# Local attention two heads at a time, normalised only by the head norm, and gated products in idle accumulator banks, in the mixing stages of a two-block kernel

## The reference

```python
for l in range(2):
    h = rms_norm(x, norm_mix_g[l])
    p = h @ w_in[l]
    y_a = silu(layer_norm(causal_conv(p[..., :256] * sigmoid(p[..., 256:o1]))))   # 31 taps
    q, k, v = heads(p[..., o1:o2])                    # 4 heads of 64
    y_b = causal_softmax(q @ k.T / 8) @ v             # one block of 256: plain causal attention
    y_b = y_b * rsqrt(mean(y_b**2, per head) + 1e-6) * moba_out_g[l]
    y_c = gla_chunked(...)                            # gated linear attention, 4 heads of 128
    y_c = y_c * rsqrt(mean(y_c**2, per head) + 1e-6) * gla_out_g[l] * silu(p[..., o6:])
    x = x + concat(y_a, y_b, y_c) @ w_out[l]
    x = x + ffn_with_short_conv(rms_norm(x, norm_ffn_g[l]), ...)
```

## Time and profile before

| | us |
|---|---|
| median of 3 runs (1288.66 to 1292.35) | 1292.04 |
| the profiled execution | 1291.89 |
| its span | 1290.2 |
| PE busy in it | 1255.8 |
| DVE busy | 820.3 |
| ACT busy | 670.9 |
| POOL busy | 144.6 |

### The profile page before, as it was taken

One profiled execution on the slowest core, in us unless ns is written; L12 is line 12 of the kernel. 1 busy time (PEld: TensorE's weight loads), 2 busy tenths in 40 slices (PEclk: granted clock), 3 DMA queues, 4 the chain that ended last, 5 costly groups with the idle time before them and its releaser, 6 DMA issues.

```text
span 1290.2 us, 16634 instructions
## 1 busy us (share of the span) xinstructions
PE 1255.8 (97%) x6276; PEld 1032.7 (80%) x6276; DVE 820.3 (64%) x943; ACT 670.9 (52%) x794; POOL 144.6 (11%) x169
## 2 busy tenths in 40 slices
PE   6999999999999999999989999999999999999997
PEld 5888888888898678888878778888888877888885
DVE  4466455545567665555459877877746987677762
ACT  6554254444455554444346365676526554767651
POOL 2000000000010000000019510000004931000000
PEclk9999999999999999999989999999999999999999
DMA  8544554446364235555523325544562423544440
GB/s 327 219 155 182 184 195 180 171 174 225 131 245 164 95 145 201 195 194 213 196 94 141 132 97 196 195 159 167 196 225 107 164 99 131 196 183 162 177 179 33
DMA packets 31526, 220.13 MB, mean 171 GB/s; under 512 B 3888, under 2 KB 3920, under 8 KB 5488
## 3 DMA queue, kind: packets, MB, share of 16 engines
q1 hardware_dynamic: 29664, 213.92, 44.8%
q0 software_dynamic: 1664, 5.41, 1.3%
q10 hardware_dynamic: 144, 0.04, 0.0%
HBM read 218.30 MB, written 1.05 MB: 170 GB/s over the span
## 4 chain that ended last, share of the span: by engine, by line
PE 92%; DVE 5%; ACT 2%; POOL 1%; issue 1%; DMA 0%; POOLq 0%; ACTq 0%
PE acc L1440 26%; PE acc L1442 26%; PE acc L1441 26%; PE tb L1468 5%; DVE wlo L899 2%; PE acc L1617 1%; PE acc L1619 1%; PE acc L1620 1%; ACT whi L473 1%; DVE cacc L1225 1%; PE tb L1831 1%; PE tb L1531 1%; PE tb L1652 1%; PE tb L1857 0%; PE tb L1671 0%
## 5 line engine op out<-in xcount | busy, mean ns | idle before, releaser
L899 DVE TENSOR_TENSOR wlo<-raw,whi 128x2048 fp32r<-128x2048 f32 x202 | 462.7, 2310 | 240.0 <-ACT whi L473 240.0
L473 ACT ACTIVATE whi<-raw 128x2048 fp32r<-128x2048 f32 x202 | 380.6, 1907 | 110.2 <-PE acc L1442 100.9
L1440 PE MATMUL acc<-whi,xth 128*128 128x512 f32 (+1 forms) x1056 | 419.4, 397 | 8.2 <-DVE wlo L899 6.2
L1442 PE MATMUL acc<-whi,xtl 128*128 128x512 f32 (+1 forms) x1056 | 410.1, 388 | 0.0
L1441 PE MATMUL acc<-wlo,xth 128*128 128x512 f32 (+1 forms) x1056 | 409.3, 388 | 0.0
L1440 PEld LDWEIGHTS acc<-whi,xth 128*128 128x128 f32 x1056 | 199.2, 189 | 53.3 <-issue 8.3
L1442 PEld LDWEIGHTS acc<-whi,xtl 128*128 128x128 f32 x1056 | 199.1, 189 | 41.4
L1441 PEld LDWEIGHTS acc<-wlo,xth 128*128 128x128 f32 x1056 | 199.5, 189 | 37.4
L1440 PE MATMUL acc<-whi,yth 128*128 128x512 f32 x512 | 203.8, 398 | 1.8 <-DVE ytl L1373 1.8
L1442 PE MATMUL acc<-whi,ytl 128*128 128x512 f32 x512 | 200.1, 391 | 0.0
L1441 PE MATMUL acc<-wlo,yth 128*128 128x512 f32 x512 | 199.9, 390 | 0.0
(11 more groups left out here) (230 smaller groups left out, 1005.4 us busy)
## 6 DMA issues: line engine op xcount, KB each, us to landing
raw<-in_stream SPq DMA_DIRECT2D x202, 1024.0 KB, 4.8
rb<-in_rel_rows POOLq DMA_DIRECT2D x8, 256.0 KB, 2.9
x<-in_x_in SPq DMA_DIRECT2D x2, 512.0 KB, 5.8
gs_sb<-in_gs_row POOLq DMA_DIRECT2D x1, 1024.0 KB, 5.5
frow<-in_fin_row POOLq DMA_DIRECT2D x2, 512.0 KB, 5.1
out<-x SPq DMA_DIRECT2D x2, 512.0 KB, 2.6
ws_sb<-in_ws_t POOLq DMA_DIRECT2D x1, 512.0 KB, 4.2
gb_sb<-in_gate_b POOLq DMA_DIRECT2D x2, 128.0 KB, 3.0
```

The costliest lines, as they stand in the source:

```text
L473: act.activation(whi[:, s, :], raw[:, s, :], ACT.Copy).then_inc(hi_ready, 1)
L899: dve.tensor_tensor(wlo[:, s, :], raw[:, s, :], whi[:, s, :], ALU.subtract).then_inc(lo_ready, 1)
L1440: pe.matmul(o, xh, wh, start=first, stop=False)
L1442: return pe.matmul(o, xl, wh, start=False, stop=last)
```

## The change

In both mixing layers:

- **Scores.** The attention goes by pairs of heads, p = 0 and 1. Two heads lie in rows 0 to 63 and 64 to 127 of `mqT`/`mkT`; `moba_scores` alternates between them and writes to two banks, and each DVE instruction, each pair of maxima and each copy then covers two heads. There are two scores places on PE instead of four.
- **No division.** The exponentials are not divided by their sums. The four heads' products lie side by side in `tb[0]`; ACT squares the bank (line 811 of the new file), DVE sums per head, adds EPS times the squared sum of exponentials, POOL takes the root, and one DVE multiply per layer makes `mo`.
- **Banks.** `gla_out(0)` and `gla_out(1)` go to the accumulators of step 4, which are idle then, one right after the other; `y_turn` uses two banks of its own.
- **Order.** The weight splits `lo(U0+11)` and `lo(U0+12)` come later on DVE; the attention is over before `out_product`; unit j = 1 waits for all three remainders instead of two; `mo_turn` stands between units 1 and 2 instead of within unit 2; on ACT the copy of the attention's high part stands ahead of `hi(U0+14)` and `hi(U0+15)` instead of behind them.

```diff
+        pp2 = [at("pp2_0", [2, 384], o_sc + 2112), at("pp2_1", [2, 384], o_sc + 1088)]
+        tball = ctx.enter_context(nc.psum_tensor("tb", [P, 4, 512], F32))
...
                 keep(4, mv, 256)
                 hi(U0 + 11)
-                h_exp(0)
+                moba_exp(0)
                 o_keep(0)
-                h_keep(0)
+                o_keep(1)
+                moba_exp(1)
                 hi(U0 + 12)
+                moba_keep(0)
...
-                o_keep(1)
-
+                keep(5, rs, 512, ACT.Silu, (0,))
                 act.wait_ge(x_sl, 2 * l + 2)
                 act.activation(yth[:, 0:512], ycs[:, :, :].rearrange("p a t -> p (a t)"), ACT.Copy).then_inc(x_yh, 1)
-                keep(5, rs, 512, ACT.Silu, (0,))
-                h_exp(1)
+                moba_keep(1)
+                act.wait_ge(t_o, 2 * l + 2)
+                act.activation(msq[:, :], tb[0], ACT.Square).then_inc(t_sq, 1)
                 keep(5, rs, 512, ACT.Silu, (1,))
...
-                lo(U0 + 11)
...
+                def moba_begin(p):
+                    i = 2 * l + p
+                    dve.wait_ge(t_s, i + 1)
+                    w, b = pp2[p][:, :, :], cmask[:, :].unsqueeze(1).to_broadcast([P, 2, 2 * P])
+                    dve.scalar_tensor_tensor(w[:, :, 0:P], tb12[:, :, 0:P], float(DH) ** -0.5, b[:, :, P:2 * P],
+                                             ALU.mult, ALU.add)
...
+                moba_begin(0)
                 for m in range(M):
                     dve.wait_ge(x_ltr, l + 1)
...
+                moba_begin(1)
                 dve.wait_ge(x_lr, l + 1)
...
-                lo(U0 + 12)
+                lo(U0 + 11)
...
+                lo(U0 + 12)
...
+                dve.wait_ge(x_or, l + 1)
+                gated(0)
+                y_gain(0)
...
+                gated(1)
+                y_lo(0)
+                y_gain(1)
+                dve.wait_ge(t_r, l + 1)
+                dve.tensor_tensor(mo[:, :, :].rearrange("p m (h d) -> p (m h) d", d=DH),
+                                  tb[0].rearrange("p (c d) -> p c d", d=DH),
+                                  stat[:, 120:128].unsqueeze(2).to_broadcast([P, 8, DH]), ALU.mult).then_inc(t_y, 1)
+                y_lo(1)
                 lo(U0 + 13)
...
+                def moba_scores(p):
+                    if p:
+                        pe.wait_ge(t_sb, 2 * l + p)
+                    else:
+                        pe.wait_ge(x_mcp, 2 * l + 2)
+                    for m in range(M):
+                        for h in range(2):
+                            r = slice(DH * h, DH * h + DH)
+                            mm = pe.matmul(tb[1 + h][:, P * m:P * (2 * m + 1)], mqT[r, p, P * m:P * m + P],
+                                           mkT[r, p, 0:P * (m + 1)], start=True, stop=True)
+                    mm.then_inc(t_s, 1)
...
-                step(5, m0={1: lambda: state_inc(5), 3: all_of((state_inc, (6,)), (first_scores, ())),
-                            5: all_of((ln_turn, ()), (gla_out, (0,)))},
-                     end=lambda: h_t(0),
-                     m1={1: all_of((gla_out, (1,)), (ln_back, ())), 5: all_of((first_pv, ()), (second_scores, ()))})
-                h_s(2)
+                step(5, m0={1: lambda: state_inc(5), 3: all_of((state_inc, (6,)), (moba_scores, (0,))),
+                            5: all_of((ln_turn, ()), (gla_out, (0,)), (gla_out, (1,)))},
+                     end=lambda: moba_scores(1),
+                     m1={2: ln_back, 3: lambda: moba_turn(0), 5: all_of((moba_pv, (0,)), (moba_turn, (1,))),
+                         7: lambda: moba_pv(1)})
...
-                        pe.wait_ge(x_yl, 4 * l + (1, 2, 3, 4)[j])
+                        pe.wait_ge(x_yl, 3 * l + (1, 3, 3)[j])
...
-                    (0, 0): lambda: h_t(1), (0, 1): all_of((h_v, (1,)), (y_turn, (0,))), (0, 2): lambda: y_turn(1),
-                    (0, 3): all_of((h_s, (3,)), (h_t, (2,))), (1, 0): lambda: h_v(2),
-                    (1, 1): all_of((pe.wait_ge, (x_yl, 4 * l + 3)), (h_t, (3,))), (1, 2): lambda: h_v(3),
-                    (2, 2): mo_turn})
+                    (0, 0): lambda: y_turn(0), (0, 3): lambda: y_turn(1), (1, 3): mo_turn})
```

More of the change, by code:

```diff
@@ L197, in two_blocks_kernel @@
         og = at("og", [M, 512], o_sb + 1664)
[L198 to L199 removed]
+        pt2 = at("pt2", [6 * P], o_sb + 2688)
         ptap = at("ptap", [SEQ], o_sc + 8768)
@@ L413, in _, with head_root @@
             final_root(FIN1, 0)
[L414 to L421, removed]
+            def head_root(l):
+                pool.wait_ge(x_oss, l + 1)
+                pool.tensor_scalar(stat[:, 80:88], stat[:, 96:104], 1.0 / DV, EPS, ALU.mult, ALU.add).then_inc(x_oms, 1)
+                pool.wait_ge(x_oms, l + 1)
+                pool.tensor_tensor(stat[:, 112:120], stat[:, 80:88], mhalf[:, 0:8], ALU.pow).then_inc(x_or, 1)
             for l in range(2):
@@ L638, in y_hi @@
                 act.activation(yth3[:, 8 + p, :], tb[3][:, SEQ:2 * SEQ], ACT.Copy).then_inc(w_hi, 1)
[L640 to L656, removed]
             act.wait_ge(n_r, STATS[2] + 1)
@@ L1372, in _ @@
-                dve.wait_ge(x_yh, 4 * l + 4)
-                dve.tensor_tensor(ytl[:, 512:1024], xg[:, 0, :], yth[:, 512:1024], ALU.subtract).then_inc(x_yl, 1)
+                dve.wait_ge(x_or, l + 1)
+                gated(0)
+                y_gain(0)
+                den = stat[:, 240:248]
+                dve.wait_ge(t_p, 8 * (l + 1))
+                dve.scalar_tensor_tensor(stat[:, 248:256], den, EPS, den, ALU.mult, ALU.mult).then_inc(t_d2, 1)
+                dve.wait_ge(t_sq, l + 1)
+                dve.tensor_reduce(stat[:, 256:264], msq[:, :].rearrange("p (c d) -> p c d", d=DH), AX.X,
+                                  ALU.add).then_inc(t_ms, 1)
@@ new lines, in _ @@
+                y_lo(1)
+                lo(U0 + 13)
+                dve.wait_ge(t_tr, l + 1)
+                dve.tensor_tensor(xg[:, 0, :].rearrange("p (a t) -> p a t", t=SEQ),
+                                  tb[2].rearrange("p (a t) -> p a t", t=SEQ),
+                                  mog[:, l, :].unsqueeze(2).to_broadcast([P, 2, SEQ]), ALU.mult).then_inc(t_g, 1)
+                dve.wait_ge(t_hi, l + 1)
+                dve.tensor_tensor(ytl[:, 512:1024], xg[:, 0, :], yth[:, 512:1024], ALU.subtract).then_inc(t_lo, 1)
@@ new lines, in moba_turn @@
+                def moba_turn(p):
+                    pe.wait_ge(t_p, 4 * (2 * l + p) + 4)
+                    if p:
+                        pe.wait_ge(t_ptc, 2 * (2 * l + p))
+                    else:
+                        pe.wait_ge(t_sb, 2 * l + 2)
+                    for i in range(6):
+                        o = tb[1][:, P * i:P * i + P] if i < 4 else tb[2][:, P * (i - 4):P * (i - 3)]
+                        mm = turn(o, pp2[p][:, i // 3, P * (i % 3):P * (i % 3) + P])
+                        if i in (3, 5):
+                            mm.then_inc(t_pt, 1)
@@ new lines, in moba_pv @@
+                def moba_pv(p):
+                    pe.wait_ge(t_ptc, 2 * (2 * l + p) + 2)
+                    for h in range(2):
+                        pt, c = 3 * P * h, DH * (2 * p + h)
+                        v = [mv[:, kk, c:c + DH] for kk in range(M)]
+                        pe.matmul(tb[0][:, c:c + DH], pt2[:, pt:pt + P], v[0], start=True, stop=True,
+                                  skip_group_check=True)
+                        pe.matmul(tb[0][:, 256 + c:256 + c + DH], pt2[:, pt + P:pt + 2 * P], v[0], start=True, stop=False,
+                                  skip_group_check=True)
+                        mm = pe.matmul(tb[0][:, 256 + c:256 + c + DH], pt2[:, pt + 2 * P:pt + 3 * P], v[1], start=False,
+                                       stop=True, skip_group_check=True)
+                    mm.then_inc(t_o, 1)
```

201 lines of the change are left out of this document (67 added, 134 removed).

## The result

| | before | changed |
|---|---|---|
| median, 20 executions each | 1291.85 | 1294.9 |
| lowest and highest | 1288.66, 1292.51 | 1289.15, 1296.12 |
| span of the profiled execution | 1290.2 | 1293.7 |
| PE busy in it | 1255.8 | 1256.3 |
| DVE, ACT, POOL busy | 820.3, 670.9, 144.6 | 814.5, 660.9, 139.4 |

The ratio is 1.002 with a 95% interval of 1.0014 to 1.0027: by 3 us the changed kernel is the slower one, which is surely more than nothing and less than the 0.3% that the prediction takes as its bound for "the same". The forecast was 1293.5, within 1288.3 to 1297.0. The nearness is in part luck: it hides two errors of opposite kinds, which the trace shows one by one.

What follows compares the result with a forecast made beforehand. PE's own work was taken as the bound (92% of the time). Per layer -2.6 - 2.0 + 1.15 + 0.8 + 0.6 + 2.45 + 0.3 = +0.7 us, +1.4 for both: median 1292.04 to 1293.5, range 1288.3 to 1297.0.

Steps and rivals of the forecast that it cites:

- (a): PE's two waits in the mixing stage, for normalised `mo` and its remainder `ytl`, go: -2.6 us per layer.
- (b): Two of four scores places on PE disappear, priced at 1.0 us each: -2.0 us per layer, bounds 1.7 to 2.1.
- (c): `gla_out(1)` loses its wait for a copy, and table loads and small DVE instructions go: no time gained.
- (g): Unit j = 1 waits on PE for the third remainder, made out of `y_turn(1)` directly ahead: +2.45 us per layer.
- (h): Last three units: ACT's attention copy ahead of `hi(U0+14)` delays the splits, so PE waits ahead of unit 3: +0.3 us per layer.
- (d): PE waits at `ln_back` for `cvn`, behind the second pair's masks and maxima on DVE: +1.15 us per layer.
- (e): PE waits at `moba_pv(1)` for ACT's second-pair copies `pt2`, with a silu table load on the path: +0.8 us per layer.
- (f): PE waits at `y_turn(0)` for DVE's convolution remainder, `lo(U0+12)` and gating of four heads: +0.6 us per layer.
- the residual add's wait of 0.75: PE's wait for the residual add after the last units was to stay as it is: 0.0 change per layer.
- The pause lets the clock fall: Rival: the 2.5 us pause ahead of unit 1 halves PE's clock, losing 1.7 us; 1295.2 one layer, 1296.9 both; chance 0.2.
- Covered hand-overs: Rival: PE's five new hand-overs cost nothing (1282.9) or half (1288.2); chance 0.14 for any time below 1288.2.
- Halves that do not overlap: Rival: a pair's scores on PE cost twice one head's, so the scores saving becomes 0: 1297.5 us; chance 0.04.

Runs made afterwards that it cites:

- experiment 4: Changed kernel with pair scores head after head, with both heads read from the same row half, or with the first pair at two places: 1294.97, 1294.51, 1298.15 us.
- the two filled kernels, experiment 2: Changed kernel with 18 or 9 discarded transposes on PE behind `y_turn(1)`, inside the wait ahead of unit 1: 1291.47 and 1291.96 us.
- Experiment 3: Changed kernel with DVE's `cvn` ahead of `moba_begin(1)`, ACT's `hi(U0+12)` ahead of `moba_exp(1)`, or both moves: 1295.24, 1293.87, 1290.33 us.
- all_orders: Changed kernel with unit 1's wait split and statements moved earlier on DVE (`cvn`, `lo(U0+11)`, `lo(U0+12)`, `lo(U0+14)`) and ACT (`hi(U0+12)`, `hi(U0+14)`): 1282.77 us.
- the kernel before with fillers: Kernel before the change plus discarded transposes: 15 ahead of the first mixing layer's step 0, 22 ahead of the first block's seventh pair's transposes: 1290.87 us.
- cvn_and_hi12: Changed kernel with both DVE's `cvn` moved ahead of `moba_begin(1)` and ACT's `hi(U0+12)` moved ahead of `moba_exp(1)`: 1290.33 us.

## Why the prediction came out as it did, step by step

**What was right.** The terms are per layer. (a) -2.6: both waits gone, no other in their place. (b) -2.0, bounds 1.7 to 2.1: a place costs the same with one head as with two (experiment 4), but 0.88 and not 1.0, so two are 1.76. The whole agrees: the first scores to the norm's transpose are 778.53 - 727.76 = 50.77 us, 49.15 without the fall, against 776.91 - 728.07 = 48.84 before; with the other terms as measured this leaves -1.8 for (b). (c) 0: nothing is seen. (g) 2.45, "the largest term and the surest": PE's next matmul comes 2.86 us after `y_turn(1)`, just the 2.87 of the earlier trace rows, and 2.26 of it is shown as wait. (h) 0.3 was 0.25: 0.48 us from the last matmul ahead of unit 3 to its first, less a step of 0.23.

**What was somewhat too large.** (d) 1.15 was 742.34 - 741.15 - 0.23 = 0.96. DVE has `cvn` begun 2.96 us after S and not 3.14. (e) 0.8 was 0.57 and (f) 0.6 was 0.39: the pieces were there at S + 11.1 and S + 14.4 and not at 11.4 and 14.7, and most of this is the 0.2 us by which ACT had the second exponentials done earlier (S + 4.25, not 4.45). The terms written for (e) add up to 11.65 and not to the 11.4 that is used; the trace takes 6.83 us for that chain on ACT (742.59 to 749.42) where they have 7.2, since each activation starts about 0.1 us before the shown end of the one before it. Of the rest, the residual add's wait of 0.75 stayed (0.79 by the same reckoning, 778.53 - 777.51 - 0.23). Together with (b) the sum is +0.3 us per layer where the prediction has +0.7. The table load was again followed by the next activation at once; here is ACT ahead of (e):

```profile
745.26 1.28 ACT L804 ACT_TABLE_LOAD   x1
746.55 1.02 ACT L804 ACTIVATE ycs<-tb,cln 128x256 f32<-128x256 f32 x2
749.03 0.39 ACT L783 ACTIVATE pt<-tb 128x256 f32<-128x256 f32 x1
```

It takes 1.28 us and the silu starts 0.01 us after it. The Trainium skill (ScalarE: Activation LUTs, "What ACT_TABLE_LOAD costs") counts a drain of about 1.38 us more; by that page, as an estimate, (e) would have been near 2 us. The trace has 0.57 and does not bear it out.

**What was wrong.** The step that failed is the choice between forecast and rival. "The pause lets the clock fall" had 0.2, with the right cause, place and price (1.7 us against 1.62 measured), and with both layers 1296.9. It happened in both layers of the profiled execution, and in 8 of the 14 layers of all kernels profiled here that have this pause of 2.26 us (layer 0 in 6 of 7 kernels, layer 1 in 2 of 7). The argument for leaving it out was that the pause "lies between the one that was followed by a fall and the one that was not, nearer to the first"; by that very sentence it should have been the likeliest case. The prediction also passed over a row of the kernel before: behind the pause of 2.02 us at 656.89, shorter than the new one, the clock is 0.55 and then 0.77. Without a fall the sum as measured gives 1291.85 + 2 x 0.31 = 1292.5, and the two filled kernels, 1291.5 and 1292.0, are near it. With both it gives 1295.7. The median of 1294.9 lies between, nearer to both. The forecast of 1293.5 came within 1.4 us because 0.8 us too much in the sum stood against 2.4 us of clock that it left out; so far it was luck.

**The other rivals.** Covered hand-overs: no, each was there. Halves that do not overlap: no, a pair takes 0.86, and 1.50 with both heads in one half. Experiment 3 shows what the sum does not say: hand-overs behind one another are not independent terms. For the forecast adding them was fair, since each was computed with those before it in place; for asking what a repair of one is worth it was not (0, 0.17 and 1.20).

## What to carry to other kernels

Before counting what a change saves on the engine that bounds, walk the new order once per hand-over and ask which engine stood idle earlier and could have had the piece ready; here DVE stood idle for 5.7 us and ACT for 3.3 ahead of a piece that was then late, and moving five statements and splitting one wait turned 3 us slower into 9 us faster. A producer's wait written for the last of several parts is worth splitting where the consumer takes them in order; here it gave 4.1 us per layer. And a pause of 2 us or more can be dearer than its length: give the half clock behind it a price and a chance, or fill the pause.

## What the runs showed of the hardware

**The same pause is not always followed by the same clock.** The wait of 2.02 us for `xtl` at 656 is followed by a low clock in the profiles of the kernel before and of the changed one, and in `all_orders` by none:

```profile
655.00:660.00 5.00, 3.98 (x22) 3.43 (x23) 3.02 (x4) 0.66 (x2) 2.20 (x4) 1.00 0.21 43
```

The pause of 2.95 us at 453 in the kernel before with fillers has 1.00 behind it too, where the earlier trace rows has 0.66:

```profile
450.00:455.00 5.00, 2.05 (x13) 1.64 (x12) 3.10 (x5) 0.87 (x2) 0.00 (x0) 1.00 0.45 134
```

Over the 14 profiled executions, the program's first 20 us aside, pauses of 2.92 to 2.96 us were followed by a fall in 13 of 14 cases, those of 2.02 in 11 of 12, those of 2.26 in 8 of 14, and those of 1.71 to 1.76 (14) and of 1.28 to 1.34 (6) in none. So length alone does not order them (the pause of 2.02 comes 1.1 us behind one of 1.50). Nor is the price one number: behind 2.26 it was 1.6 us, behind 2.02 it was 1.55 to 2.85, by the time from the pause to the first scores (68.66 without a fall, 70.2 to 71.5 with one).

Of the kernels with the pause of 2.26, only `cvn_and_hi12` had no fall behind it in either layer; there PE had waited less ahead of it (0.45 us since the second scores, against 1.25 to 1.46 in the others). Its other ten executions speak against chance: they end at 1290.9 at most, the profiled one at 1291.19, and one more fall of 1.6 would put that at 1292.8. But what in the two moves keeps the clock up was not tested. The 20 times of the changed kernel lie in three groups 3 us apart (two at 1289.2, three at 1292.1 to 1292.4, fifteen at 1294.5 to 1296.1), which is about two falls of 1.6 each; which falls they are is not seen. The Trainium skill (TensorE: Matmul & The Clock Gate, "The HAM clock gate") has an idle array drop to half clock. The runs agree that idleness brings the fall (experiment 2), and add that for a pause of 2 to 3 us it is a chance to be priced, not a rule.

**Neighbouring instructions in different row halves overlap whatever their order**: the scores of two heads take 0.86 us with the heads in turn and one after the other, and 1.50 in the same half (experiment 4).
